# The router's scores by tokens: h as the stationary side, two banks, no copy and no transposes

## The reference, cut to what matters

```python
scores = jax.nn.sigmoid((xf @ w_router).astype(jnp.float32))   # (256, 1024) @ (1024, 64)
biased = scores + b_router.astype(jnp.float32)
grouped = biased.reshape(T, N_GROUPS, N_EXPERTS // N_GROUPS)
group_score = jnp.sum(lax.top_k(grouped, 2)[0], axis=-1)
...                                                             # 4 of 8 groups, then 8 experts
_, idx = lax.top_k(jnp.where(expert_mask, biased, NEG_INF), TOP_K)
w = jnp.take_along_axis(scores, idx, axis=-1)
...
routed = jax.ops.segment_sum(...)                               # the chosen experts, weighted
shared = swiglu(xf, ws1, ws3, ws2)                              # one expert for all tokens
return (routed + shared).reshape(B, S, D)
```

## Time and profile before

| | before |
|---|---|
| timed runs: median (lowest to highest of 3) | 2399.28 us (2398.68 to 2400.83) |
| profiled execution, own time | 2398.06 us |
| its span | 2396.8 us |
| PE busy | 2309.0 us (96%) |
| PE weight loads busy | 1650.0 us (69%) |
| DVE, ACT, POOL busy | 814.2, 570.1, 135.6 us |
| moved by DMA | 673.21 MB, mean 281 GB/s |

### The profile page before, as it was taken

One profiled execution on the slowest core, in us unless ns is written; L12 is line 12 of the kernel. 1 busy time (PEld: TensorE's weight loads), 2 busy tenths in 40 slices (PEclk: granted clock), 3 DMA queues, 4 the chain that ended last, 5 costly groups with the idle time before them and its releaser, 6 DMA issues.

```text
span 2396.8 us, 34579 instructions
## 1 busy us (share of the span) xinstructions
PE 2309.0 (96%) x14027; PEld 1650.0 (69%) x14027; DVE 814.2 (34%) x2133; ACT 570.1 (24%) x1231; POOL 135.6 (6%) x179
## 2 busy tenths in 40 slices
PE   7999999999998998999999999998989999999998
PEld 4868897676665665768887676666657777854764
DVE  0376623212121111486524122211223544421264
ACT  2234412111111112224211111111113343321264
POOL 4040000000000000100000000000000000000110
PEclk9999999999999999999999999999999999999999
DMA  9785684999999996855776999999993543141110
GB/s 336 273 294 190 228 338 188 408 418 417 417 418 418 418 418 256 309 180 191 285 300 242 407 418 420 418 418 417 418 375 121 182 156 110 71 150 53 71 71 18
DMA packets 194619, 673.21 MB, mean 281 GB/s; under 512 B 14000, under 2 KB 50072, under 8 KB 144528
## 3 DMA queue, kind: packets, MB, share of 16 engines
q1 hardware_dynamic: 187776, 656.87, 70.5%
q0 software_dynamic: 6240, 13.99, 1.7%
q10 hardware_dynamic: 432, 0.01, 0.0%
HBM read 661.38 MB, written 9.45 MB: 280 GB/s over the span
## 4 chain that ended last, share of the span: by engine, by line
PE 88%; DMA 7%; DVE 1%; ACT 1%; issue 1%; SPq 1%; DVEq 0%; ACTq 0%
PE ps L282 49%; PE ps L2175 13%; PE ps L2212 7%; DMA ring<-in_w 7%; PE ps L2228 4%; PE ps L1757 3%; PE ps L1207 1%; PE ps L695 1%; PE ps L2924 1%; PE ps L3537 1%; DMA ring<-in_w_in 1%; PE ps L3702 1%; PE ps L3685 1%; PE ps L2198 1%; PE ps L3694 1%
## 5 line engine op out<-in xcount | busy, mean ns | idle before, releaser
L282 PE MATMUL ps<-hT,ring 128*128 128x256 f32 (+2 forms) x2352 | 541.1, 386 | 3.2 <-ACT ar L1577 1.9
L282 PEld LDWEIGHTS ps<-hT,ring 128*128 128x128 f32 (+1 forms) x2352 | 438.5, 189 | 99.7 <-issue 37.1
L2175 PE MATMUL ps<-ring,ar 128*32 128x256 f32 (+2 forms) x2688 | 314.3, 389 | 8.6 <-DMA ar<-in_w 4.7
L2175 PEld LDWEIGHTS ps<-ring,ar 128*32 128x32 f32 (+2 forms) x2688 | 189.1, 126 | 96.8 <-issue 20.4
L2175 PE MATMUL ps<-ar 128*64 128x256 f32 (+2 forms) x1120 | 179.5, 388 | 9.1 <-DMA ring<-in_w 9.1
L2212 PE MATMUL ps<-ring,ar 128*64 128x512 f32 (+2 forms) x728 | 159.7, 612 | 12.6 <-DMA ring<-in_w 7.3
L2495 DVE TENSOR_TENSOR ar<-ar,ps 128x256 f32<-128x256 f32 x50 | 21.1, 422 | 437.0 <-PE ps L2175 437.0
L2519 DVE SCALAR_TENSOR_TENSOR exact_parts<-ps,ar,exact_parts 128x512 fp32r<-128x512 f32 x100 | 75.1, 751 | 215.0 <-ACT exact_parts L2363 209.4
L282 PE MATMUL ps<-ring,ar 128*128 128x512 f32 x320 | 140.3, 595 | 0.0
L2363 ACT ACTIVATE exact_parts<-ps,ar 128x512 fp32r<-128x512 f32 x100 | 68.7, 687 | 291.0 <-PE ps L2212 272.8
L2175 PEld LDWEIGHTS ps<-ar 128*64 128x64 f32 (+2 forms) x1120 | 102.7, 129 | 46.2 <-issue 11.8
(11 more groups left out here) (461 smaller groups left out, 2813.8 us busy)
## 6 DMA issues: line engine op xcount, KB each, us to landing
ring<-in_w SPq DMA_DIRECT2D x259, 1024.0 KB, 21.1
ar<-in_w SPq DMA_DIRECT2D x100, 1024.0 KB, 18.5
ring<-in_w_mod SPq DMA_DIRECT2D x36, 2048.0 KB, 11.9
ring<-in_w_in SPq DMA_DIRECT2D x28, 2048.0 KB, 12.0
ring<-in_ab_w_in SPq DMA_DIRECT2D x46, 1024.0 KB, 11.3
cst<-in_w SPq DMA_DIRECT2D x25, 1024.0 KB, 18.0
ring<-in_w_out SPq DMA_DIRECT2D x4, 2048.0 KB, 10.1
ar<-in_ab_w_in SPq DMA_DIRECT2D x8, 1024.0 KB, 24.5
```

Of the source, the lines that this page charges most:

```text
L282: ins = te.matmul(o, l, r, start=(first and i == 0), stop=(last and i == len(pairs) - 1), skip_group_check=lax)
L2175: ins = te.matmul(b[cols, 0:256], K.x_b[:, kk, in_pair(p, cols)], w[r][:, kk, :], start=(kk == 0), stop=(kk == 7))
```

## The change

The two sides of the router's product change places: `h` is now stationary, in two halves i of 128 tokens, and the router's weights (64 columns) are moving. The result has tokens in the partitions and experts in the columns at once, one bank for each half (7 and 6), both taken before the router starts. The copy to SBUF, the two transposes and PE's wait for the copy go away; the sigmoid reads the two banks, in two instructions of 64 columns where there was one of 128.

```diff
-    rb = yield from K.bank(("logits", l), only=7)
+    rb = []
+    for i in range(2):
+        rb.append((yield from K.bank(("scores", l, i), only=7 - i)))
     te.wait_ge(*(yield ("ring", "router", l)))
     for kk in range(8):
         te.wait_ge(*(yield ("h", ("ffn", l), kk, 0)))
-        ins = te.matmul(rb[0:64, 0:256], w[:, kk, :], h[:, kk, :], start=(kk == 0), stop=(kk == 7))
-    ins.then_inc(*K.pe("logits_ps", l, ps=rb))
+        for i in range(2):
+            ins = te.matmul(rb[i][:, 0:64], h[:, kk, i * P:(i + 1) * P], w[:, kk, :], start=(kk == 0), stop=(kk == 7))
+    ins.then_inc(*K.pe("logits_ps", l))
     K.pe.also("used", "router", l)
+    for i in range(2):
+        K.ps["logits_ps", l, i] = rb[i]
...
-        if j == 0:
-            rb = yield from K.bank(("scores", l), only=6)
-            te.wait_ge(*(yield ("logits", l)))
-            for i in range(2):
-                ins = te.transpose(rb[:, i * 64:(i + 1) * 64], K.t_b[0:64, i * P:(i + 1) * P], K.ident[0:64, 0:64])
-            ins.then_inc(*K.pe("logits_turned", l, ps=rb))
...
     ac.wait_ge(*(yield ("logits_ps", l)))
-    ac.activation(K.t_b[0:64, :], K.ps["logits_ps", l][0:64, 0:256], ACT.Copy).then_inc(*K.act("logits", l))
-    ac.wait_ge(*(yield ("logits_turned", l)))
-    ac.activation(K.sc, K.ps["logits_turned", l][:, 0:128].rearrange("p (i e) -> p i e", i=2),
-                  ACT.Sigmoid).then_inc(*K.act("scores", l))
+    for i in range(2):
+        ac.activation(K.sc[:, i, :], K.ps["logits_ps", l, i][:, 0:64], ACT.Sigmoid).then_inc(*K.act("scores", l, i))
...
-    ve.wait_ge(*(yield ("scores", l)))
+    ve.wait_ge(*(yield ("scores", l, 1)))
```

## The result

| | before | after |
|---|---|---|
| median (lowest to highest of 15 runs) | 2399.0 us (2395.74 to 2401.17) | 2404.01 us (2399.71 to 2407.36) |
| ratio, 95% interval | | 1.0023 [1.0016, 1.003] |
| profiled execution, own time | 2398.06 us | 2407.36 us |

The change takes a wait, a copy and two transposes out of each routing stage and makes the kernel 5.0 us slower. The forecast was 2406.3, with 0.58 on slower by over 0.2%.

The account below looks back on a forecast made before the run. TensorE, busy 96% of a 2396.8 us span, was taken as the bound. A slower router and shared products, less the 0.49 us saved, gave 3.5 us a layer: 2399.3 + 7.0 = 2406.3 us, 8-in-10 range 2398.0 to 2410.

Parts of the forecast that it names:

- The clock under the new router: Routing stage: TensorE stays at half clock through the router and 3.44 us of shared products; stage ends 3.5 us later.
- Rival A: Router: full clock returns inside it, after 3.4 us as with wide products; -0.2 us a layer, 2398.9 in all; chance 0.30.
- The delay: End of the shared products, each layer: 393.85 against 390.34 in layer 0, 3.5 us later, saving included.
- The pitch: Router's 32 instructions: 0.116 us apart at full clock, doubled to 0.232 at half clock, 7.42 us in all.
- 3.44 + 11.96 = 15.40: Shared products after the router: eight at half clock for 3.44 us, the other 56 at full clock for 11.96.
- The 0.49 for the removed wait and transposes: TensorE between the first 16 shared products and the next: dropping wait and two transposes saves 0.49 us a layer.
- In both layers: Router start in layers 0 and 1: the clock falls there because of the idle stretch ahead; two layers give +7.0 us.
- The removed wait, transposes and copy; ACT and DVE: Routing stage: 64 shared products run without a gap; ScalarE and VectorE work costs nothing, with 6.5 us of cover.
- B, the DMA stream: Expert loop: TensorE's waits for weights swallow the delay, leaving none at the end, 2399.3 us; chance 0.06.

Follow-up runs that it names:

- e1: Changed kernel with each router instruction moving the 64 weight columns twice (128 columns, second copy unused), same weight loads: 2398.6 us, ratio 0.9999.
- e2: Changed kernel with the router's products put behind the first 8 shared products instead of ahead of them: 2398.01 us, ratio 0.9997.
- e3: Changed kernel with 10 unused 256-column product instructions on constants while TensorE waits for the norm: 2395.29 us, ratio 0.9987.
- e4: Kernel before with 10 unused 256-column product instructions on constants while TensorE waits for the norm: 2395.86 us, ratio 0.9993.
- e7: Kernel before run again, unchanged, for a second profiled execution: 2398.5 us, ratio 1.0002.
- e6: Changed kernel run again, unchanged, for a second profiled execution: 2404.42 us, ratio 1.0025.
- e5: Kernel before with 16 unused 256-column product instructions per layer between the shared products and the transposes of h: 2403.45 us, ratio 1.0029.

## Why the prediction was right, step by step

**The clock under the new router** decided the sign, as forecast: low through the router and into the shared products. Rival A, the clock returning inside the router, is refuted by the windows above, and e1 and e2 show that it is the narrow products, not the swap itself, that keep it low: with 128 columns moved per load, or behind wide products, the loss is gone. e3 shows it from the other side: with the clock held at its full level the changed kernel loses nothing. Why narrow products do not bring the clock back, no run here shows. A rested on the clock coming back after the same time behind narrow products as behind wide ones. Behind the wide ones of the earlier trace rows and e2 it was back after 3.4 us; narrow ones here ran for 6.8 us without a pause and had not brought it back.

**Where sizes were off.** The delay was put at 3.5 us a layer and is 2.7 (22.50 - 19.81). Two terms made that. The pitch: at half clock I doubled the 0.116 of ten short products to 0.232; the 32 weight loads in the timeline after start (377.17 - 370.39) / 32 = 0.212 us apart, 0.64 us less a layer. At full clock e3 gives (371.29 - 367.73) / 32 = 0.111. No run shows the 0.107 at the lower end of rival A's range as the pitch of these products; e3's 0.111 stands in its place. Half of the 0.212 is 0.106, which is near the 0.107 of the expectations of e2 and e3. Most of the rest is in the shared products: from 377.28 to 392.54 they took 15.26 us, where 3.44 + 11.96 = 15.40 was worked out, the clock returning at 380.5, 3.25 us after their start and not 3.44. The 0.49 for the removed wait and transposes reads 0.60 with the clock held (14.48 in e4 from the first shared product to the last, 13.88 in e3). In rival A's range the upper end, at a pitch of 0.135, comes out at 2400.1 and not 2400.4; nothing hangs on it.

**"In both layers."** That the clock falls at the router's start, because of the idle stretch ahead, I took as given from one execution. It isn't given: e7's layer 0 shows the kernel before without it, though PE was idle ahead of it as well (busy 0.00 us from 366.90 to 369.05). With the idle stretch filled (e3, e4) the clock fell in none of four stages; with it left, ahead of the router or within it in eight of the ten of both kernels. The forecast held because the new router did not escape in the two executions traced: in e6's layer 0 the clock did not fall before it, but in its middle. That part is luck: the rows of one execution could not show it. Nor is it shown for every execution: of e6's eight timed runs one took 2397.72 us, 0.5 above the kernel before's median there.

**The removed wait, transposes and copy; ACT and DVE.** As predicted: 64 shared instructions without a break, the scores' chain off the path.

**B, the DMA stream.** Refuted, by the changed kernel's trace and by e5. SP's issue moved with the shared products' end, from 390.75 to 392.95, the DMA engines being idle before it as in the earlier trace rows (timeline, and windows, of the changed kernel). PE's longest wait for weights kept its length (28.76 us, last line below, from the chain of waits, against 28.61 in the earlier trace rows), so stream and PE shifted together:

```profile
392.95 0.80 SPq L579 DMA_DIRECT2D ring<-in_w  x2
```

```profile
384.00:391.00 7.00, 7.00 (x34) 6.17 (x33) 1.64 (x9) 0.38 (x1) 0.00 (x0) 1.00 0.01 2
```

```profile
714.42 28.76 DMA ring<-in_w
```

The reason given, that the delay goes through because it also holds back SP's issue, is not the whole of it: in e5 the issue was not held back, and the delay went through all the same.

In all, 7.0 us were forecast, 5.5 stand in the two stages, and 5.0 in the medians.

## What to carry to other kernels

Swapping the sides of a product to save a copy and a transpose also changes what the stream on TensorE looks like: narrow moving sides behind wide loads, right after an idle wait, can leave the engine at half clock for the work behind them too (10.2 us in three of the changed kernel's four stages), which costs more than the transposes did (the stage 2.7 us longer, where it is 0.48 shorter with the clock held). Putting such products behind wide ones (e2) or filling the idle wait ahead (e3) took the loss away; moving columns twice for nothing was faster than moving them once (2398.6 us against 2404.01). A clock's fall seen in one execution has to be looked for in a second before it is counted on.

## What the runs showed of the hardware that was not expected

The granted clock fell while PE was busy without a break. e6 shows it with narrow products (PE busy 1.85 of 1.85 us ahead of the fall at 370.5); in the second block of the changed kernel it fell amid eight instructions that move 512 columns past weights of 4 columns in 16 partitions (windows, then timeline):

```profile
1828.00:1835.00 7.00, 7.00 (x25) 3.55 (x24) 2.11 (x3) 2.92 (x5) 0.00 (x0) 0.97 0.68 196
1835.00:1841.70 6.70, 6.70 (x15) 4.29 (x14) 0.00 (x0) 0.91 (x1) 0.00 (x0) 0.52 0.33 111
```

```profile
1828.37 3.72 PE L2921 MATMUL ps<-hT,ring 128*128 128x256 f32 x16
1832.02 4.46 PE L2802 MATMUL ps<-ar,cst 16*4 16x512 f32 x8
```

PE was busy 7.00 of 7.00 us ahead of it. By an estimate from the pitches at half and at full clock (0.427 against 0.2135 us in the kernel before), the stretch of 6.8 us costs 3.4, half of its length. The kernel before has a shorter one at that place in its second execution (e7):

```profile
1829.00:1832.30 3.30, 3.30 (x9) 2.58 (x9) 0.00 (x0) 0.14 (x1) 0.00 (x0) 0.50 0.42 147
```

Of the nine traces only the first one of the kernel before has no such stretch there: it lasts 6.8 us in the first and second of the changed kernel, in e1 and in e4, which is the kernel before with the filler (from 1821.6 to 1828.4), and 3.4 us in e2, e3, e5 and e7. So it goes with neither kernel, and a single pair of traces would have put 3.4 us of it down to the change. What sets its length was not tried.
